# A two-layer streaming encoder step: keys and values of two head groups projected as one job of 512 columns, and the jobs around them put in another order

## What is computed

```python
def _sb_core(q, k, v, qpos, kpos):
    z = jnp.einsum('bqhd,bkhd->bhqk', q, k).astype(jnp.float32) * (SB_HD ** -0.5)
    valid = kpos[None, :] < qpos[:, None]
    log_beta = jax.nn.log_sigmoid(z)
    log_rem = jnp.where(valid, jax.nn.log_sigmoid(-z), 0.0)
    later = lax.cumsum(log_rem, axis=3, reverse=True) - log_rem
    a = jnp.where(valid, jnp.exp(log_beta + later), 0.0).astype(v.dtype)
    return jnp.einsum('bhqk,bkhd->bqhd', a, v)

def _odd_layer(x, pos, caches, prm):
    w_in, w_out, ln_g, ln_b = prm
    q, k, v, g = _split_cols(x @ w_in, (SB_W, SB_W, SB_W, SB_W))
    ...
    o = (o.reshape(b, s, SB_W) * jax.nn.silu(g)) @ w_out
    y = _layernorm(ALPHA * x + o, ln_g, ln_b)
    return y, (k, v)
```

## Time and profile before

| | |
|---|---|
| median of 3 runs | 856.92 us (855.97 to 858.75) |
| the profiled execution | 856.7 us, its span 854.9 us |
| PE busy | 826.6 us, 97% of the span |
| DVE busy | 524.8 us, 61% |
| ACT busy | 412.8 us, 48% |
| PEclk | 9 (tenths of full speed, 9 is 90% or more) in all slices but the last |
| DMA | mean 101 GB/s |

### The profile page before, as it was taken

One profiled execution on the slowest core, in us unless ns is written; L12 is line 12 of the kernel. 1 busy time (PEld: TensorE's weight loads), 2 busy tenths in 40 slices (PEclk: granted clock), 3 DMA queues, 4 the chain that ended last, 5 costly groups with the idle time before them and its releaser, 6 DMA issues.

```text
span 854.9 us, 17106 instructions
## 1 busy us (share of the span) xinstructions
PE 826.6 (97%) x6676; PEld 706.4 (83%) x6676; DVE 524.8 (61%) x1048; ACT 412.8 (48%) x945; POOL 74.8 (9%) x102
## 2 busy tenths in 40 slices
PE   7999999999999999999999999999999999999995
PEld 6996688888888888768899998889888878887674
DVE  4175346655565647756942465666666766778777
ACT  4333433334354455532234556675566665687710
POOL 3020001000000000000220011001100110121002
PEclk9999999999999999999999999999999999999998
DMA  7631211211332334414133334233332433334113
GB/s 236 153 98 51 62 44 57 64 44 38 96 99 88 109 108 138 152 51 148 56 113 105 119 106 130 87 92 125 122 99 79 136 114 116 122 119 146 52 38 123
DMA packets 67534, 86.25 MB, mean 101 GB/s; under 512 B 6017, under 2 KB 53921, under 8 KB 67457
## 3 DMA queue, kind: packets, MB, share of 16 engines
q1 hardware_dynamic: 63712, 74.47, 28.4%
q0 software_dynamic: 3744, 10.70, 4.0%
HBM read 74.25 MB, written 10.90 MB: 100 GB/s over the span
## 4 chain that ended last, share of the span: by engine, by line
PE 81%; issue 9%; DVE 4%; ACT 4%; POOL 2%; DMA 0%; DVEq 0%; SPq 0%; POOLq 0%; ACTq 0%
PE turn L952 24%; PE pair L952 17%; PE value L952 16%; PE proj L952 15%; PE turn L992 3%; PE turn L1168 2%; POOL rstd L925 1%; PE value L992 1%; PE proj L992 1%; PE proj L1168 1%; DVE w_lo L1598 1%; ACT w_hi L1368 1%; PE pair L992 1%; DVE probs L1710 0%; PE value L1168 0%
## 5 line engine op out<-in xcount | busy, mean ns | idle before, releaser
L1598 DVE TENSOR_TENSOR w_lo<-stage,w_hi 128x512 fp32r<-128x512 f32 (+1 forms) x136 | 91.9, 683 | 118.2 <-ACT w_hi L1368 117.8
L952 PE MATMUL turn<-w_hi,xT_hi 128*128 128x256 f32 (+2 forms) x340 | 106.0, 312 | 0.9 <-DVE xT_lo L1603 0.6
L952 PE MATMUL turn<-w_hi,xT_lo 128*128 128x256 f32 (+2 forms) x340 | 102.5, 301 | 0.0
L952 PE MATMUL turn<-w_lo,xT_hi 128*128 128x256 f32 (+2 forms) x340 | 102.4, 301 | 0.0
L1368 ACT CAST w_hi<-stage 128x512 fp32r<-128x512 f32 (+1 forms) x144 | 87.4, 616 | 20.6 <-PE value L952 6.4
L952 PEld LDWEIGHTS turn<-w_hi,xT_hi 128*128 128x128 f32 x340 | 64.8, 191 | 3.6 <-DVE x_sb L1840 1.4
L952 PEld LDWEIGHTS turn<-w_hi,xT_lo 128*128 128x128 f32 x340 | 64.8, 191 | 2.4
L952 PEld LDWEIGHTS turn<-w_lo,xT_hi 128*128 128x128 f32 x340 | 64.9, 191 | 2.1
L1710 DVE TENSOR_TENSOR_SCAN probs<-probs 128x512 f32<-128x512 f32 (+4 forms) x80 | 61.5, 801 | 1.7
L1448 ACT ACTIVATE work<-pair,peak 128x512 f32<-128x512 f32 (+4 forms) x80 | 40.9, 516 | 44.5 <-DVE peak L1699 44.4
L952 PE MATMUL value<-w_hi,xT_hi 128*128 128x256 f32 (+2 forms) x194 | 60.5, 312 | 0.4 <-DVE w_lo L1598 0.4
(11 more groups left out here) (528 smaller groups left out, 2079.1 us busy)
## 6 DMA issues: line engine op xcount, KB each, us to landing
stage<-in_w_in_odd_dram SPq DMA_DIRECT2D x64, 256.0 KB, 2.7
stage<-in_w_in_even_dram SPq DMA_DIRECT2D x44, 256.0 KB, 2.8
k_c<-in_cache_sb_k_dram SPq DMA_DIRECT2D x32, 256.0 KB, 3.4
v_c<-in_cache_sb_v_dram SPq DMA_DIRECT2D x32, 256.0 KB, 2.9
mlaK<-in_cache_diff_k_dram SPq DMA_DIRECT2D x8, 512.0 KB, 4.1
mlaK<-in_cache_diff_v_dram SPq DMA_DIRECT2D x8, 512.0 KB, 4.3
stage<-in_w_out_even_dram SPq DMA_DIRECT2D x16, 256.0 KB, 2.6
stage<-in_w_out_odd_dram SPq DMA_DIRECT2D x16, 256.0 KB, 2.6
```

The source lines that it names most:

```text
L952: return nc.tensor.matmul(o, l, r, start=first, stop=last)
L1598: v.tensor_tensor(piece(w_lo[:, sec % 2, words]), piece(stage[:, n % STAGES, :]), piece(w_hi[:, sec % 2, words].bitcast(F32)), ALU.subtrac ...
```

## The change

`JOINT = (1, 2)`: for groups 1 and 2 the jobs `k` and `v` of a tile become one job `kv`. Its matmuls stream 512 columns, 256 from each of the two slots of `w_hi` or `w_lo`, so there are 24 of them where there were 48. It reads both sections at once, so both must be converted before it, and neither slot is free until the fifth `kv` job is done. Drained is told only after ACT's second copy. For groups 1 to 3 the sections come in the order q, k, v, g (before: k, v, g, q for groups 0 to 2, and k, v, q, g for group 3). The conversion of v's section comes as four quarters in a row behind the last query job, that of g's section as four in a row behind the last `kv` job. Each of the 12 steps gets one hand-set list of bundles in groups 1 and 2; group 3 keeps single `k` and `v` jobs and `share`. The gate chain of groups 1 and 2 starts with their second gate job and ends in the next group's steps.

```diff
-COST = {"k": 2.9, "v": 2.9, "q": 3.5, "g": 3.5, "out": 2.8, "kT": 0.25, "xT": 0.5}
+COST = {"kv": 5.5, "k": 2.9, "v": 2.9, "q": 3.5, "g": 3.5, "out": 2.8, "kT": 0.25, "xT": 0.5}
...
-    SECTIONS += [f"{_kind}{_g}" for _kind in ("kvgq" if _g + 1 < GROUPS else "kvqg")]
+    SECTIONS += [f"{_kind}{_g}" for _kind in ("qkvg" if _g else "kvgq")]
...
+    def gate_chain(g):
+        return [(kind, g, blk) for blk in range(2) for kind in ("sig", "sigm", "silu", "silum")]
+
+    def four(kind, g, coming):
+        return beside([[(kind, g, blk, part)] for blk in range(2) for part in range(2)], convert(coming))
...
     def project(g):
...
+        fill = four("q", g, f"k{g}")
+        coming = convert(f"v{g}")
+        if g in JOINT:
+            both = [[("kv", g, 0)]] + [[("kv", g, t), ("kT", g, t - 1)] for t in tiles[1:]]
+            fill[-1] += coming[:3] + [("gblocks", g)] + coming[3:]
         else:
...
+            both = beside([[("k", g, 0)]] + [[("k", g, t), ("kT", g, t - 1)] for t in tiles[1:]], coming)
+            fill[-1].append(("gblocks", g))
+            both += beside([[("v", g, t)] for t in tiles], convert(f"g{g}"))
+        if g > 1:
+            for bundle, job in zip(fill + both, gate_chain(g - 1)[3:]):
+                bundle.append(job)
+        if g not in JOINT:
+            both[5].append(("kT", g, S_TILE))
+            return share(fill + both, [ROOM[s] for s in ("3", "0", "S", "2", "1", "S", "3", "0", "S", "2", "1", "S")])
+        coming = convert(f"g{g}")
+        both[-1] += coming[:3] + [("kT", g, S_TILE)] + coming[3:]
+        gates = four("g", g, f"q{g + 1}")
+        for bundle, job in zip(gates[1:], gate_chain(g)):
             bundle.append(job)
...
+        return [fill[:1], fill[1:3], fill[3:]] + [[bundle] for bundle in both + gates]
...
+                elif kind == "kv":
+
+                    _, g, t = job
+                    for h in range(2):
+                        wait_drained(pe, ("xT", 1, t, h))
+                    wait_bank(pe, job)
+                    o = ps(job)[:, :].rearrange("p (s c) -> p s c", s=2)
+                    for k in range(KD):
+                        for sec in sections_of(job):
+                            wait_quarter(job, sec, k // 2)
+                        cols = slice(k * HALF, (k + 1) * HALF)
+                        m = product(o, x_block(k, tok(t)), (w_hi[:, :, cols], w_lo[:, :, cols]), k == 0, k == KD - 1)
+                    m.then_inc(done, 1)
...
+                    if kind != "v":
+                        n = kn_no[job] - 1
+                        if n >= 2:
+                            act.wait_ge(stored_kn[n % 2], 16 * (n // 2))
+                        i = nc.scalar.copy(k_n[:, n % 2, :], ps(job)[:, columns(job, "k")])
+                    if kind != "k":
...
+                        i = nc.scalar.copy(v_n[:, g % 2, t, :], ps(job)[:, columns(job, "v")])
+                    i.then_inc(done, 1)
```

More of the change, by code:

```diff
@@ new lines, in gate_chain, with project0 @@
+    def gate_chain(g):
+        return [(kind, g, blk) for blk in range(2) for kind in ("sig", "sigm", "silu", "silum")]
+    def four(kind, g, coming):
+        return beside([[(kind, g, blk, part)] for blk in range(2) for part in range(2)], convert(coming))
+    def project0():
+        keys = [[("k", 0, 0)] + layer1(2) + [("ln", 0, S_TILE)], [("k", 0, 1), ("kT", 0, 0)] + layer1(3) + [("shift", 0, S_TILE)],
+                [("k", 0, 2), ("kT", 0, 1)], [("k", 0, 3), ("kT", 0, 2)]]
+        values = [[("v", 0, t)] for t in tiles]
+        fill = beside(keys, convert("v0"))
+        fill += [values[0], [("kT", 0, 3)] + layer1(S_TILE) + values[1], [("k", 0, S_TILE)]]
+        values[2] += [("kT", 0, S_TILE)]
+        fill += beside(values[2:], convert("g0"))
+        gates, queries = four("g", 0, "q0"), four("q", 0, "q1")
+        for bundle, job in zip(gates[1:] + queries, gate_chain(0)):
+            bundle.append(job)
+        return fill + gates + queries + [[("gblocks", 0), ("silum", 0, 1)]]
@@ L308, in project @@
             bundle.append(job)
-        return fill + gates + queries + [[("gblocks", g), ("silum", g, 1)]]
-    jobs += flat_jobs(project(0))
+        return [fill[:1], fill[1:3], fill[3:]] + [[bundle] for bundle in both + gates]
+    jobs += flat_jobs(project0())
     steps, fills = [], []
@@ L366, in sections_of @@
         return [f"G{job[1] // 2}"]
+    if kind == "kv":
+        return [f"k{job[1]}", f"v{job[1]}"]
     if kind in ("k", "v", "q", "g"):
@@ L660, in trunk_kernel, with keys_of, values_of, columns @@
         subln_no = ordinal(("gd",), lambda j: j[2] == 1)
-        kn_no = ordinal(("k",))
+        kn_no = ordinal(("k", "kv"))
+        def keys_of(g, t):
+            return ("kv" if g in JOINT else "k", g, t)
+        def values_of(g, t):
+            return ("kv" if g in JOINT else "v", g, t)
+        def columns(job, kind):
+            first = GW * (SECTIONS.index(f"{kind}{job[1]}") % 2) if job[0] == "kv" else 0
+            return slice(first, first + GW)
         blocks_no = ordinal(("qblocks", "gblocks"))
@@ L1293, in _ @@
                     project(job, t)
+                elif kind == "kv":
[10 more added lines that the diff above has]
+                    m.then_inc(done, 1)
                 elif kind == "kT":
                     _, g, t = job
-                    wait_drained(pe, ("k", g, t))
-                    transposes(job, [(i * P, k_n[:, (kn_no[("k", g, t)] - 1) % 2, i * P:(i + 1) * P]) for i in range(2)])
+                    wait_drained(pe, keys_of(g, t))
+                    transposes(job, [(i * P, k_n[:, (kn_no[keys_of(g, t)] - 1) % 2, i * P:(i + 1) * P]) for i in range(2)])
                 elif kind in ("q", "g", "G"):
```

52 lines of the change are left out of this document (13 added, 39 removed).

## The result

The change makes the kernel slower: 868.46 us, median of 4 runs (865.37 to 870.58), against 856.98 us (855.97 to 858.75, 4 runs); the ratio is 1.0129, interval 1.0094 to 1.0164. I forecast 863.4, slower with a chance of 0.73, and a range of 856 to 869. The sign and the mechanism held; the loss is 11.5 us where I had worked out 6.7, and the median lies inside the stated range but above the forecast's own one, 859.3 to 866.6. The profiled execution took 870.58 us, its span 868.8.

A forecast was written before the change was run, and what follows sets the result against it. TensorE's own instructions plus its waits were taken to bound the stretch from 482 to 765 us. New waits 14.8, old waits -4.6 and wide jobs -3.5 gave +6.7 on 856.7: 863.4 us, range 856 to 869.

The forecast's parts named there:

- wide jobs: Joint `kv` jobs of groups 1 and 2: 0.35 us saved for a tile, -3.5 us for ten tiles.
- waits of before: From 482 to 765 us: TensorE's seven old waits for the drain of `turn2` go, -4.6 us.
- `sig`, step 9: Groups 0 and 1: `bsT` waits 2.1 us for `turn`'s drain, which stands behind `sig` on ACT; twice, +4.2 us.
- `silum`, step 0: Groups 1 and 2: `silum` stands ahead of `turn2`'s drain, moved there from step 9; 1.3 us each, +2.6.
- last key transposes: Directly behind those of tile 3, TensorE waits 0.65 us for the `kv` bank's two copies; twice, +1.3.
- burst of g: Step 7: the gate job waits 0.95 us for the fourth quarter of g's section, loaded late; twice, +1.9.
- burst of v: Step 2: the `kv` job waits for v's first and third quarters, then the second `cacheT`; +1.65 and +1.4, 3.1 us.
- group 2: Conversions, `gblocks` and `silu` ahead of drains in steps 3, 6 and 9 of group 2, +1.7 us.
- rival 5: The granted clock falls in the new waits from 482 to 765 us: +8.5 us, 872; chance 0.04.
- rival 3: The wide job gives nothing, its two pieces streaming as two matmuls: 866.9 us; chance 0.07.
- Rival 2: A late step shortens the next wait, so new waits are 5.5 to 10.7 us: 854.1 to 859.3; chance 0.14.
- Rival 4: The loads that the four bursts hang on land late: +7.6 us, 871; chance 0.08.

The follow-up runs named there:

- e9: Changed kernel with fourth stage buffer, last key transposes and gate chain behind the turns, group 3's sections in old order; 855.36 us, ratio 0.9981 to the kernel before.
- e10: Group 3 in old order and gate chain behind the turns, but single key and value jobs and three stage buffers; 855.18 us, 0.9982 to the kernel before.
- e2: Changed kernel with `sig` put behind the drains of `turn` and `turn2` at step 9 of groups 0 and 1; 864.44 us, ratio 1.0079 to the kernel before.
- e3: Changed kernel with a fourth stage buffer for weights from q's section of group 1 on; 865.27 us, ratio 1.0082 to the kernel before.
- e4: Changed kernel with each joint job's matmuls as 48 of 256 columns; 876.65 us, ratio 1.0226 to the kernel before.
- the first experiment: The changed kernel measured again, nothing altered, also called e1; 868.49 us, ratio 1.0129 to the kernel before.
- e6: Changed kernel with the key transposes of tile 4 put behind the `turn` of step 7; 870.31 us, ratio 1.0148 to the kernel before.

## Why the prediction was right, and what it missed

The terms against the changed kernel's trace, each bracket read as it stands (the prediction put at 0.09 us what a bracket leaves out):

| term | forecast | measured |
|---|---|---|
| wide jobs | -3.5 | -3.3 (5.57 against 5.90 for two jobs of the earlier trace rows, ten tiles); -3.8 by the sums of e9 and e10, where single jobs take 2.95 to 3.05 |
| waits of before | -4.6 | -4.1 in brackets, |
| `sig`, step 9 | +4.2 | 2.21 twice |
| `silum`, step 0 | +2.6 | 1.13 twice |
| last key transposes | +1.3 | 0.52 twice |
| burst of g | +1.9 | 1.42 and 0.91 |
| burst of v | +3.1 | 0.51, 0.68, 0.48; 0.41, 0.94 |
| group 2 | +1.7 | 0.67, 0.37, 0.32, 0.47, 0.37 |
| first `cacheT` of step 6 | not counted | 0.17 twice |

**What was right.** Seventeen of the twenty waits came at their places, with the releaser named; the two of step 6 and a score of group 2 that waits 0.47 us for `stick` were not foreseen. All twenty are 15.6 us in brackets, for 14.8 forecast. Laying the old durations along the new order gave `sig` to about 0.1 us each. Experiments 2 and 3 took two of the terms away singly, and 4 confirmed the price of the wide job: rows 5, of matmuls with one contiguous operand of 512 columns, stood for the two pieces. The Trainium skill ("TensorE: Matmul & The Clock Gate", Back-to-back issue gap) gives an isolated matmul a gap of N / 2.4 + 2.5 ns, from which I estimate a saving of 0.6 us for ten tiles. The matmuls of 512 columns stand 227 ns apart here, those of 256 119 to 123, where the formula has 216 and 109, and the measurement decides.

**What was missed,** 4.8 us by the medians. First, the waits: 0.8 us more in brackets than forecast, 0.47 of it the `stick` that I had costed at nothing; and I added 0.09 to each old wait and nothing to the twenty new ones, 1.8 us by that estimate. That is a plain error of the sum. Second, TensorE's own time behind the reordering: I costed the move of blocks at nothing, and `turn` and `turn2` went from 16.86 to 18.77 us over the ledger's stretch. Of these 1.9, 0.34 are the two waits of step 6, and 1.6 are left. With these terms, 15.6 + 1.8 - 4.6 - 3.8 + 1.6 = 10.6, the ledger of the first experiment, whose clock held, is explained (10.5 over before); the first profile has 3.0 more.

Third, the clock, rival 5, which I priced at 8.5 us and 0.04. Its mechanism came true in part: not through the share of idle time, as I had it, but behind single waits of about 2 us, and for 0 to 3 us. The Trainium skill (the same page, A second HAM failure mode: psum-queue depth-cycling) has, for another kernel, of bf16 matmuls of 512 columns, the clock oscillate when TensorE idles briefly and often between groups of matmuls as the banks are cycled. The traces agree only in part. Waits for a bank of the ring did precede the drop to 0.52: in the five profiles with the two waits of 2.2 us (the first one, e1, e3, e4, e6) the clock fell behind seven of the ten. But of the many waits of up to 1.6 us, over all the profiles, it fell behind one (e4, where 1.53 and 0.27 stand close together), and before, with eight of up to 1.1, it held.

**What was luck.** The forecast's own range, 859.3 to 866.6, was missed by 1.9 us. The median lies in the stated one, 856 to 869, by half a microsecond, and that range went so far up to cover rival 3, in which the wide job gives nothing. That isn't what happened: the wide job gives 3.3 to 3.8 us, and the excess came from the terms above. The sign in the last paragraph of the prediction, that busy time which doesn't fall would speak against the wide matmul, was a bad one too: PE is busy for 829.2 us, and for 826.4 in the first experiment, against 826.6 before, with the wide job at its forecast 5.57. Busy time counts modelled ends; between e10 and e9 it falls by 2.0 us where the starts of the products give 3.8.

Rival 2, that a late step makes the next wait shorter, has a real effect that my sum took as small: e6 shows it for one pair, e2 gives 3.7 of 4.4. Rival 4 (loads land late) came in part: the third quarter of v's burst was too late in the steps of group 0 in every trace of joint jobs with three buffers, and the number of cuts in that job changed from one execution to another.

## What to carry to other kernels

When jobs on an in-order queue are merged, list for each merged place what now stands ahead of each PSUM drain, and lay the known durations along it. Here this gave the waits behind known durations (`sig`, `silum`, the key transposes) to 0.1 to 0.2 us, and those behind a load to about 0.5. Put chains that nobody waits for behind the drains, and count the buffers before turning spread loads into a burst: here the bursts of four wanted a fourth buffer. And give the old kernel every repair that the new one gets; here that took away the whole case for the wide jobs, which save what they promise and give it back in waits and in what follows what on TensorE.

## What the runs showed of the hardware that I had not expected

- Behind eight of eleven waits of TensorE of 1.9 to 2.2 us the granted clock fell, to 0.50, and matmuls ran at the lower level for 3 to 4 us, once in e4 for nearly 7 (a 128x256 one every 0.213 us for 0.119, a 128x320 one every 0.267 for 0.147). That cost 1.5 us where I counted it, and more at that place of e4 (0.50 from 565 to 570). The same two waits in another execution of the same kernel left it at 1.00. What decides it is open.
- 48 matmuls of 256 columns in one job take 5.83 us (e4), two jobs of 24 take 5.90, 24 of 512 columns 5.57: the width gives 0.27, the join 0.07.
- The three transposes of a sample step's `turn` take 0.42 us ahead of a `value` product with a stationary of 64 columns (e9) and 0.25 ahead of a projection (e10).
